# Both MLPs of a two-layer decoder trunk in block jobs of seven products

## The reference

```python
hn = rms_norm(h, mlp_norm[i])                        # h: 1024 x 1024
h = h + jnp.square(jax.nn.relu(hn @ w_mlp_in[i])) @ w_mlp_out[i]     # 1024 x 4096, 4096 x 1024
hn = rms_norm(h, ple_norm[i])
h = h + (p[i] @ w_ple_up[i]) * jax.nn.sigmoid(hn @ w_ple_gate[i])
```

## Time and profile before

| | us |
|---|---|
| three runs | 2553.98, 2552.82, 2546.62 |
| median | 2552.82 |
| span of the profiled execution (its own total isn't given) | 2544.6 |
| TensorE busy | 2446.6 (96%) |
| VectorE busy | 1154.1 (45%) |
| GpSimd busy | 816.7 (32%) |
| ScalarE busy | 553.0 (22%) |

### The profile page before, as it was taken

How to read it: one execution, slowest core, us unless ns; L and a number is a source line. 1 busy time by engine, 2 the same in 40 slices (tenths; PEclk the granted TensorE clock), 3 DMA queues, 4 the chain that set the end, 5 groups by cost and what they waited for, 6 DMA issues and landing times.

```text
span 2544.6 us, 32593 instructions
## 1 busy us (share of the span) xinstructions
PE 2446.6 (96%) x13054; PEld 1987.8 (78%) x13054; DVE 1154.1 (45%) x1173; ACT 553.0 (22%) x854; POOL 816.7 (32%) x492
## 2 busy tenths in 40 slices
PE   8998967999999999999998999999999999999997
PEld 6887856888888888888886776678888888888886
DVE  6867278432422423325527355552432332423625
ACT  3120255212011011021213245622001011011215
POOL 4433112233332233333232343643333233333231
PEclk9998978999999999999999999999999999999998
DMA  7372332211111111111213111211111111111211
GB/s 210 105 116 83 104 107 60 99 50 49 43 49 49 49 49 49 44 46 50 66 50 100 36 32 50 58 42 50 44 47 49 49 49 49 46 44 50 66 50 66
DMA packets 249192, 159.66 MB, mean 63 GB/s; under 512 B 32164, under 2 KB 236168, under 8 KB 249096
## 3 DMA queue, kind: packets, MB, share of 16 engines
q1 hardware_dynamic: 235560, 139.69, 19.1%
q10 hardware_dynamic: 13552, 18.81, 2.9%
HBM read 131.81 MB, written 25.49 MB: 62 GB/s over the span
## 4 chain that ended last, share of the span: by engine, by line
PE 88%; DVE 8%; issue 1%; ACT 1%; ACTq 1%; DMA 0%; POOL 0%; DVEq 0%; SPq 0%; POOLq 0%
PE ps L624 70%; PE ps L1139 3%; PE ps L775 2%; PE ps L1171 2%; PE ps L1099 1%; DVE hg_queries_keys L1934 1%; PE ps L1112 1%; PE ps L1123 1%; PE ps L1062 1%; PE ps L796 1%; PE ps L811 1%; PE ps L691 1%; DVE s_state L1662 1%; DVE stage L1592 1%; PE ps L794 1%
## 5 line engine op out<-in xcount | busy, mean ns | idle before, releaser
L487 POOL CAST w_hi<-w_raw 128x1024 fp32r<-128x1024 f32 x198 | 211.5, 1068 | 1456.8 <-PE ps L624 1133.7
L624 PE MATMUL ps<-x_hi,w_hi 128*128 128x512 f32 x1568 | 485.9, 391 | 4.8 <-issue 2.3
L489 POOL TENSOR_TENSOR w_lo<-w_raw,w_hi 128x1024 fp32r<-128x1024 f32 x198 | 479.1, 2419 | 15.8
L624 PE MATMUL ps<-x_lo,w_hi 128*128 128x512 f32 x1568 | 483.0, 389 | 0.0
L624 PE MATMUL ps<-x_hi,w_lo 128*128 128x512 f32 x1568 | 482.6, 389 | 0.0
L624 PE MATMUL ps<-mid_hi,w_hi 128*128 128x512 f32 x1200 | 369.7, 389 | 2.9 <-DVE residual L2064 1.9
L624 PE MATMUL ps<-mid_hi,w_lo 128*128 128x512 f32 x1200 | 369.5, 389 | 0.0
L624 PE MATMUL ps<-mid_lo,w_hi 128*128 128x512 f32 x1200 | 369.4, 389 | 0.0
L624 PEld LDWEIGHTS ps<-x_hi,w_hi 128*128 128x128 f32 x1568 | 293.6, 188 | 69.5 <-issue 8.2
L624 PEld LDWEIGHTS ps<-x_lo,w_hi 128*128 128x128 f32 x1568 | 294.4, 188 | 61.4
L624 PEld LDWEIGHTS ps<-x_hi,w_lo 128*128 128x128 f32 x1568 | 294.4, 188 | 61.3
(11 more groups left out here) (303 smaller groups left out, 2503.3 us busy)
## 6 DMA issues: line engine op xcount, KB each, us to landing
w_raw<-w_mlp_in_in SPq DMA_DIRECT2D x64, 512.0 KB, 4.0
w_raw<-w_mlp_out_in SPq DMA_DIRECT2D x64, 512.0 KB, 4.0
w_raw<-w_in_even_in SPq DMA_DIRECT2D x20, 512.0 KB, 4.6
residual_dram<-residual ACTq DMA_DIRECT2D x2, 4096.0 KB, 12.5
w_raw<-w_ple_gate_in SPq DMA_DIRECT2D x16, 512.0 KB, 3.9
residual<-residual_dram SPq DMA_DIRECT2D x3, 2048.0 KB, 10.0
fqig_dram<-stage SPq DMA_DIRECT2D x11, 512.0 KB, 3.1
x_tokens<-x_in SPq DMA_DIRECT2D x8, 512.0 KB, 7.3
```

The source lines that it names most:

```text
L487: pool.tensor_copy(WH[:, b, :], RAW[:, b, :]).then_inc(S["w_hi_done"], 1)
L489: pool.tensor_tensor(WL[:, b, :], RAW[:, b, :], WH[:, b, :].bitcast(F32), ALU.subtract).then_inc(S["w_ready"], 1)
L624: ins = pe.matmul(acc[:, h, :], w[:, k, :], x[:, k0 + k, h * HALF:(h + 1) * HALF], start=(k == 0 and w is wh and x is xh), stop=(k == kts ...
```

## The change

Each MLP becomes 32 jobs. A job covers 256 output features, all 1024 tokens and 1024 features of the contraction. It is a product of 2x2 blocks: the contraction is split into its even and its odd tiles (four each), the outputs into two tiles of 128, the tokens into two halves of 512. The classical way has eight block products; a form of Strassen's has seven (`SLOTS = 7`), of sums and differences of blocks. One block product is 4 tiles of the contraction x 3 passes = 12 matmuls on 512 columns, into one bank. Sixteen jobs (`UP`) make all 4096 hidden features, sixteen more go over them in four chunks for the output.

What each engine does now:

- **SyncE** loads the weights of a job (1 MB) into `st_raw`, two buffers; stores the seven activation blocks of each hidden job (`mid_sums`, 1.8 MB) to DRAM; and four times per MLP reads back the four hidden jobs of a chunk, one block (1 MB) after each product of the job ahead.

```diff
+                    g, s = divmod(t, SLOTS)
+                    if s == 5 and g + 2 < JOBS:
+                        sp.wait_ge(S["st_lo_pool"], 3 * JOBS * i + 3 * (g + 1))
+                        if g + 2 == JOBS - 1:
+                            sp.wait_ge(S["mt_stored"], 16 * UP * (i + 1))
+                        raw(g + 2)
+                    if s == 5 and 1 <= g <= UP:
+                        sp.wait_ge(S["mt_ready"], UP * i + g)
+                        sp.dma_start(t_dram[i][g - 1], MT[:, :, :]).then_inc(S["mt_stored"], 16)
+                    gj, block_ = divmod(t - 1, SLOTS)
+                    if gj >= UP - 1 and gj % 4 == 3 and gj < JOBS - 1:
+                        c = (gj - (UP - 1)) // 4
+                        sp.wait_ge(S["st_prod"], PRODUCTS * i + t)
+                        sp.wait_ge(S["mt_stored"], 16 * (UP * i + 4 * c + 4))
+                        sp.dma_start(OPF[block_][:, 1, :, :], t_dram[i][4 * c:4 * c + 4, :, block_, :].rearrange("j p n -> p j n"))\
+                            .then_inc(x_op_loaded[block_], 16)
+                sp.wait_ge(S["st_lo_pool"], 3 * JOBS * i + 3 * (JOBS - 2))
 
```

```diff
+                def low(g, s, x):
+                    r = (SLOTS * g + s) % RINGS
+                    pool.wait_ge(S["st_hi"], PRODUCTS * i + SLOTS * g + s + 1)
+                    pool.tensor_tensor(SL[r][:, :, :], x, SH[r][:, :, :].bitcast(F32), sub).then_inc(S["st_lo_pool"], 1)
+
+                for g in range(JOBS):
+                    n_sum, n_low = 4 * (JOBS * i + g), 4 * (JOBS * i + g)
+                    pool.wait_ge(yt_raw_loaded[raw_of(g)], raw_visit(i, g))
+                    if g or i:
+                        pool.wait_ge(S["st_lo"], n_low)
+                    sum_(g, SA, quarter(g, 1, 0), quarter(g, 1, 1), add)
+                    pool.wait_ge(S["st_sum"], n_sum + 1)
+                    sum_(g, SB, SA[:, :, :], quarter(g, 0, 0), sub)
+                    low(g, 0, quarter(g, 0, 0))
+                    low(g, 3, quarter(g, 0, 1))
+                    pool.wait_ge(S["st_lo"], n_low + 2)
+                    sum_(g, SA, quarter(g, 0, 0), quarter(g, 1, 0), sub)
+                    sum_(g, SB, quarter(g, 0, 1), SB[:, :, :], sub)
+                    low(g, 6, quarter(g, 1, 1))
```

```diff
+                for g in range(JOBS):
+                    a_, b_, c_ = BANKS[g % 2]
+                    for s, o in enumerate((a_, b_, c_, a_, b_, c_, b_)):
+                        r = (SLOTS * g + s) % RINGS
+                        weights(g, s)
+                        bank(g, s)
+                        for j in range(4):
+                            operand(g, s, j)
+                            for w, x in ((SH[r], 0), (SH[r], 1), (SL[r], 0)):
+                                ins = pe.matmul(PS[:, o, :], w[:, j, :], OP[s][:, x, j, :], start=(s < 3 and j == 0 and w is SH[r] and x == 0),
+                                                stop=(j == 3 and w is SL[r]), skip_group_check=True)
+                        ins.then_inc(S["st_prod"], 1)
```

```diff
+            def x_operands(i, norm, m):
+
+                j, g = m // 2, col("mlp", KT * i + m)
+                act.wait_ge(S["h_ready"], 8 * norm + m + 1)
+                if i and m < 2:
+                    act.wait_ge(S["h_part"], 4 + 4 * m)
+                if m % 2 == 0:
+                    fn(OPF[0][:, 1, j, :], H[:, m, 0:HALF], ACT.Identity, scale=g)
+                    fn(OPF[2][:, 1, j, :], H[:, m, HALF:], ACT.Identity, scale=g).then_inc(S["op_x_scaled"], 1)
+                    first, second = 0, 2
+                else:
+                    fn(OPF[1][:, 1, j, :], H[:, m, HALF:], ACT.Identity, scale=g)
+                    fn(OPF[3][:, 1, j, :], H[:, m, 0:HALF], ACT.Identity, scale=g).then_inc(S["op_x_scaled"], 1)
+                    first, second = 1, 3
+                act.wait_ge(S["sq_used"], m + 8 * norm + CREDIT)
+                fn(SQ[:, :], H[:, m, :], ACT.Square).then_inc(S["sq_done"], 1)
+                act.wait_ge(S["op_x_scaled"], 10 * i + m + 1)
+                act.wait_ge(S["op_x_sum"], 10 * i + m + 1)
+                for s in (first, second):
+                    fn(OP[s][:, 0, j, :], OPF[s][:, 1, j, :], ACT.Copy).then_inc(S["op_cast"], 1)
...
+                def squared(g):
+                    n = UP * i + g
+                    act.wait_ge(S["q_scaled"], n + 1)
+                    for h in range(2):
+                        fn(Q[:, 2 * h:2 * h + 2, :], Q[:, 2 * h:2 * h + 2, :], ACT.Relu).then_inc(S["q_relu"], 1)
+                    if n:
+                        act.wait_ge(S["mt_stored"], 16 * n)
+                    for h in range(2):
+                        act.wait_ge(S["q_relu"], 2 * n + h + 1)
+                        fn(MT[:, 2 * h:2 * h + 4:3, :], Q[:, 2 * h:2 * h + 2, :], ACT.Square).then_inc(S["q_squared"], 1)
+
+                def cast(c, s):
+                    act.wait_ge(x_op_loaded[s], 16 * (4 * i + c + 2))
+                    for h in range(2):
+                        fn(OP[s][:, 0, 2 * h:2 * h + 2, :], OPF[s][:, 1, 2 * h:2 * h + 2, :], ACT.Copy).then_inc(S["op_cast"], 1)
```

```diff
+                def block_low(s, casts):
+                    dve.wait_ge(S["op_cast"], cb + casts)
+                    tt(OP[s][:, 1, :, :], OPF[s][:, 1, :, :], OP[s][:, 0, :, :].bitcast(F32), sub).then_inc(S["op_ready"], 1)
+
+                def late_difference():
+                    dve.wait_ge(S["op_x_scaled"], 10 * i + 9)
+                    tt(OPF[4][:, 1, :, :], OPF[5][:, 1, :, :], OPF[4][:, 1, :, :], sub).then_inc(S["op_x_sum"], 1)
+                    dve.wait_ge(S["op_x_sum"], 10 * i + 9)
+
+                def late_last():
+                    dve.wait_ge(S["op_x_scaled"], 10 * i + 10)
+                    dve.wait_ge(S["op_ready"], rb + 12)
+                    own(tt(OPF[6][:, 1, :, :], OPF[6][:, 1, :, :], OP[1][:, 0, :, :].bitcast(F32), sub))
+                    tt(OPF[6][:, 1, :, :], OPF[6][:, 1, :, :], OP[1][:, 1, :, :].bitcast(F32), sub).then_inc(S["op_x_sum"], 1)
+                    dve.wait_ge(S["op_x_sum"], 10 * i + 10)
+
+                def weight_low(n):
+                    r, s = n % RINGS, n % SLOTS
+                    if s in DVE_LOW:
+                        dve.wait_ge(S["st_hi"], sb + n + 1)
+                        tt(SL[r][:, :, :], (SB if s in (1, 5) else SA)[:, :, :], SH[r][:, :, :].bitcast(F32), sub).then_inc(S["st_lo"], 1)
...
+                def scaled(g):
+                    dve.wait_ge(S["st_ev"], ev(i, g, 5))
+                    dve.wait_ge(S["rstd_done"], norm + 1)
+                    tt(Q[:, 0, :], PS[:, BANKS[g % 2][0], :], RSTD[:, lefts], ALU.mult).then_inc(S["st_c11"], 1)
+                    tt(Q[:, 2:4, :], Q[:, 2:4, :], RSTD[:, rights].unsqueeze(1).to_broadcast([P, 2, HALF]), ALU.mult)
+                    tt(Q[:, 1, :], Q[:, 1, :], RSTD[:, lefts], ALU.mult).then_inc(S["q_scaled"], 1)
+
+                def mid_sums(g):
+                    n = UP * i + g
+                    dve.wait_ge(S["q_squared"], 2 * n + 2)
+                    tt(MT[:, 4, :], MT[:, 5, :], MT[:, 2, :], sub)
+                    tt(MT[:, 2, :], MT[:, 2, :], MT[:, 0, :], sub).then_inc(S["mt_sum"], 1)
+                    dve.wait_ge(S["mt_sum"], 2 * n + 1)
+                    tt(MT[:, 1, :], MT[:, 5, :], MT[:, 2, :], sub).then_inc(S["mt_sum"], 1)
+                    dve.wait_ge(S["mt_sum"], 2 * n + 2)
+                    tt(MT[:, 6, :], MT[:, 3, :], MT[:, 1, :], sub).then_inc(S["mt_ready"], 1)
...
+                def refill(c, s):
+                    for h in range(2):
+                        n = 14 * c + 2 * s + h + 1
+                        dve.wait_ge(S["op_cast"], cb + X_CASTS + n)
+                        tt(OP[s][:, 1, 2 * h:2 * h + 2, :], OPF[s][:, 1, 2 * h:2 * h + 2, :], OP[s][:, 0, 2 * h:2 * h + 2, :].bitcast(F32), sub)\
+                            .then_inc(S["op_ready"], 1)
```

613 lines of the change are left out of this document (405 added, 208 removed).

## The result

The changed kernel takes **2525.14 us** (median of 4 runs, 2521.44 to 2528.01) where the kernel before takes 2552.38 on the same chip (4 runs, 2546.62 to 2553.98). The ratio is 0.9898, interval 0.9881 to 0.9915: 27 us or 1.0% faster. The forecast was 2536 us.

What follows compares the result with a forecast made beforehand. TensorE's matmuls were taken to bound the kernel, all of each MLP. -174.1 + 4 + 89.6 + 25 + 37 + 2 = -16.5 us; span 2528.1 plus 8.2 gives 2536 us, own range 2515 to 2556, whole range 2495 to 2582.

Steps and rivals of the forecast that it cites:

- 1, matmuls: Both MLPs: 384 matmuls less in each, at an unchanged 0.2267 us per matmul, -174.1 us.
- 2, middle jobs: First-half jobs: the fifth product's eviction comes just in time for the seventh; 0.15 us per job, +4 us, bounds 0 and 55.
- 3, changes of operands: Four refills of activation blocks per MLP: TensorE waits for VectorE's work and GpSimd collisions, +89.6 us, bounds 41.6 and 112.
- 4, start of the first MLP: First MLP's start: operands made tile by tile and late blocks delay products, +25 us, 21 without collisions, 30 with full ones.
- 4, start of the second, with the tiles ahead: Second MLP's start and the tiles ahead, where VectorE sets the pace: +37 us, bounds 30 and 45.
- 4, ends: Both ends of an MLP wait up to a microsecond for the gate's low parts, +2 us.
- no gain where VectorE ends last: Low parts on GpSimd: three VectorE instructions of 0.65 us less per job against three collisions of up to 0.85.
- Collisions small: Rival 1: GpSimd's operations fall under evictions and VectorE's waits; 2474 us without any, about 2505 with half; chance 0.20.
- First half doesn't fit: Rival 2: between ScalarE's squares and the fifth eviction, blocked operations lengthen all 30 jobs, +56 us, 2588 us; chance 0.17.
- All covers hold: Rival 4: no cost anywhere beside the matmuls saved, 2379 us; chance 0.02.
- The clock: Rival 3: TensorE's clock falls twice in each of eight changes of operands, +27 us, 2563 us; chance 0.06.

Runs made afterwards that it cites:

- the run with four more sums: Changed kernel plus four more VectorE subtractions of 512 columns behind the four sums of every first-half job; 2598.40 us, ratio 1.0182.
- late blocks first: Changed kernel with the three late blocks' pieces made at once on ScalarE and the last block's subtractions earlier on VectorE, at an MLP's start; 2502.07 us, ratio 0.9806.
- GpSimd quiet: Changed kernel with GpSimd's sums and low parts on 8 columns instead of 512 in 8 of each MLP's last 16 jobs; 2474.61 us, ratio 0.9704.

## Why the prediction was right, and where its terms were off

The forecast of 2536 us, made of a sum of -16.5, was 11 us above the median; the profiled execution came out at -23.4, the medians at -27. The 4 us between those two stand in no term. Term by term, from the lateness:

| term | predicted | measured |
|---|---|---|
| 1, matmuls | -174.1 | -174.1 |
| 2, middle jobs | +4 | 0 |
| 3, changes of operands | +89.6 | +82.5 |
| 4, start of the first MLP | +25 | +25.5 (27.2 less the sum of squares, 1.7, in both) |
| 4, start of the second, with the tiles ahead | +37 | +34.7 (31.4, and 3.3 ahead) |
| 4, ends | +2 | +6.8 |
| not in the sum: ahead of the first MLP +2.9, between the MLPs -1.7 | | +1.2 |
| sum | -16.5 | -23.4 |

1. **Matmuls.** Held: 2688 at 0.2267 us. Weights that change with every product cost nothing that the trace shows; jobs 3 to 15 are each at 19.04 us.
2. **Middle jobs.** Right in kind. The squares were done at 9.9 us of the job, not 10.6, and two collisions were met. The eviction was done at 14.8, not 16.3. A part of that is a slip in my sum: 10.6 + 2.8 + 0.55 + 1.3 + 0.7 is 15.95, which already left 0.4 us. The room is 1.0 us, by the run with four more sums, where I had none.
3. **Changes.** The right engine and causes, and 41.2 us per MLP for 44.8. The collisions are 5.9 us of an ordinary change for 6.0. That the whole is 9.2 for 9.0 is partly luck: VectorE's own excess is 1.8 us, not 3.0, and the clock, which I had put at nothing, makes up the 1.5. The first change is 13.0, not 16.0. I called the transfers hidden, from 410 GB/s and a MB per product. That left out the store of 1.8 MB and the weights among the blocks of the first change. There they were a second bound, and it didn't show only because VectorE was longer still. The statement that GpSimd's low parts are "no gain where VectorE ends last" was too mild: they are a loss of 20 us.
4. **Start.** 25.5 for 25. The long pause ahead of the seventh product was 8.67 us (nearly 10 predicted), with the clock at 0.50 behind it, and that product began 38.1 us after the first (37.7 as I had it from the end of the last unit). What I hadn't seen: 6.1 us were lost at the fourth product already, and the fifth began at 21.3 us, not 19.5, because ScalarE's copy of the first product (`first_product`) stood behind the eight late scalings, 5 us. The tile chain had 51.9 us for seven tiles, 51.1 predicted, with steps of 6.0 to 9.2. The collisions there are what moving the low parts gave back.
5. **Ends.** Mis-sized: 3.4 us each, not 1. I counted the gate's low parts of the weights. The chain shows VectorE's lows of the operands (`x_lo`), which meet GpSimd and stand between the last evictions:

```profile
1219.31 3.41 DVE x_lo L2407
1222.72 0.60 DVE residual L2387
1223.31 4.71 DVE x_lo L2407 x2
...
1237.06 10.93 PE ps L727 x48
```

**The rivals.** Collisions small: out, they are 5.9 of 9.2 us. First half doesn't fit: out, by 1.0 us. All covers hold: out. The clock: in part. It did fall, as the stretches above show (0.62 and 0.50 in the first change, 0.63 behind the last wait of the second). In the changes 42 and 43 matmuls of the two MLPs came at half pace, 17 us together, and some 20 and 35 more at the starts. What that costs depends on where they lie. In an ordinary change they are behind the last wait and cost 1.5 us. In the last change they are inside the waits for VectorE and cost nothing: it is 9.7 us long in two experiments (late blocks first, in the first MLP; four sums more, in the second) where none was slow, as it is with twelve. In the first change nine or ten are behind the last wait, 1.8 to 2.0 us. So the clock is about 10 of the 82.5 us, not the 27 of the rival, and my sum hadn't got it.

## What to carry to other kernels

Before work is cut on the engine that bounds, make the account of the engine that feeds it in the densest stretch, not over the whole: VectorE was busy 64% of this kernel, and in eight stretches of 30 us TensorE lost 9 or more behind it. Count each GpSimd instruction beside VectorE's SBUF-to-SBUF work as VectorE time, too; here it was 0.84 us, of the 1.3 that such an instruction lasts, for 0.60 saved, and giving work back to the engine that was behind made the kernel faster. And at a phase's start let every queue do first what the longest chain needs: with the same instructions in another order 21 of 60 us came back.

## What the runs showed of the hardware

- A VectorE subtraction of 128x1024 with both inputs in SBUF took 1216 ns in the mean with GpSimd quiet, 1351 with GpSimd at its sums only, 1531 with three low parts added, 1811 with seven. GpSimd's own 512-column instructions last 1.27 to 1.30 us alone and up to 3.3 beside VectorE's, so both lose.
- Blocks of 1 MB, a store of 1.8 MB and weights together moved at 385 GB/s with the DMA share at 1.03; a transfer issued into that took up to 15 us to land, and 5.2 to 5.4 when the queues were empty.
- The granted clock was 0.50 behind a pause of 8.67 us, and also in changes of operands where TensorE was busy most of the time in pieces with pauses of at most 5 us. The same code with the same waits kept the clock in one execution and not in another (second change of operands: 7.7 us against 9.2).
- Parts of the program that didn't change wander between executions: the stretch ahead of the first MLP by 3.6 us, the one between the MLPs by 4.2 us and more. The stretch behind the second MLP was 143.2 to 143.3 us in the changed kernel and in every experiment.
